# Expert gathers issued from rolled loops with a staged index, in place of 512 written-out gathers

## The chip, the cores and the metric

The kernel runs on one core of one Trainium2 chip. A core has five engines with instruction streams of their own: TensorE (PE in the rows), VectorE (DVE), ScalarE (ACT), GpSimd (POOL) and SyncE (SP). They share the on-chip memory SBUF and 16 DMA engines, and they order their work by semaphores. The metric is the device time of one launch in microseconds; the time quoted is the median of several executions. Lower is better.

## The reference, cut to what matters

Two transformer-like blocks run in a row over 256 tokens of width 2048, all in float32. The change touches one part of the first block, a mixture of 16384 tiny experts. Each token picks 128 of them (8 heads of 16), and each expert is one row of a table `u` and one row of a table `v`:

```
def peer(x, wq, subkeys, u_tab, v_tab):
    ...
    idx = jnp.take_along_axis(cand_i, pos, axis=-1)
    gate = jax.nn.softmax(top_s, axis=-1)
    ...
    def block(args):
        xt, it, gt = args
        ue = jnp.take(u_tab, it, axis=0)
        ve = jnp.take(v_tab, it, axis=0)
        act = jax.nn.gelu(jnp.einsum('td,ted->te', xt, ue).astype(f32), approximate=False)
        return jnp.einsum('te,ted->td', (gt * act).astype(ve.dtype), ve)
```

So 256 tokens times 128 experts times two tables are gathered, rows of 2048 floats (8 KB) each. The rest (an mLSTM and an S5 mixer before it, a second block with three attention kinds and a feed-forward layer behind it) is untouched.

## The kernel before, in words

**Tiling.** The 256 tokens are two tiles (`TT` = 2, index `t`) of 128 tokens, one token per SBUF partition. One gather brings, for one of the 128 choices `n`, the row that each of the 128 tokens wants: 128 rows of 8 KB, 1.0486 MB. It is an indirect DMA issued by GpSimd, whose index column is `idx[:, t, n:n+1]`. There are four passes `q` of 128 gathers: `q` = 0 (table u, tile 0), 1 (table v, tile 0), 2 (u, tile 1), 3 (v, tile 1).

**Buffers and order.** Gather `n` goes into row buffer `n % 8` of eight buffers (`GB` = 8, `rows_`), and bumps that buffer's semaphore `row_gathered`. VectorE takes the buffers in the same order. In a u pass (called dots below, `dots_of`, L1532) it multiplies the buffer by the tile's activations and sums, with one small copy of eight results (L1536) and a wait for it behind every eight. In a v pass (called sums, `sums_of`, L1546) it adds the buffer times a weight into the accumulator `res`, each step waiting for the step before. Both are hardware loops on VectorE, eight buffers a round. Behind each buffer VectorE bumps `rows_used` (`s_free`), and GpSimd may gather into that buffer again only then: gather `n` of pass `q` waits for `q * 128 + n + 1 - 8` of them.

**What stands between.** VectorE also works out which experts are wanted (routing). The first tile's routing is in four blocks of 32 choices, and dots alternate with routing steps; the second tile's routing lies between the dots and sums of the first. Early on, GpSimd's first eight gathers use only five buffers, because the others still hold scores (`first_gathers`). Meanwhile SyncE streams a weight matrix `w_ada` that TensorE multiplies (L439), and VectorE takes the result at one place between two rounds of dots (L1652).

**GpSimd's stream.** It is written out: 512 gathers behind each other, each with its wait (L1716, called from L1720 to L1747). GpSimd does nothing else in this phase. Before a block of gathers it waits for `experts_known` (`s_idx`).

The eight-row ring is set up by these lines:

```
rows_ = [place.take(D) for _ in range(GB)]
idx = place.take(TT, HK).bitcast(U32)
dots = small[:, 32:32 + GB]
s_row = [sem(f"row_gathered{i}") for i in range(GB)]
```

Of the kernel before, what the change touches and what calls it, by code (L numbers as in the profile page):

```python
# [11 lines left out]
U32 = mybir.dt.uint32  # L12
# [17 lines left out]
def build(nc, a, out):  # L30
# [19 lines left out]
    HK = PH * TOPK  # L50
# [19 lines left out]
    with ctx:  # L70
# [5 lines left out]
        def sem(name):  # L76

            phase_sems.append(nc.alloc_semaphore(name=name))
            return phase_sems[-1]
# [16 lines left out]
        def place_at(name, words, dt=F32, at=None):  # L96
            if at is None:
                at = taken_at[0]
                taken_at[0] += words
            assert at + words <= ARENA, (name, at + words - ARENA)  # L100
            return nc.alloc_sbuf_tensor_at(name, [P, words], dt, offset=base + 4 * at), at
# [16 lines left out]
        small, _ = place_at("small", 256)  # L118
# [185 lines left out]
        for s in SECTIONS:  # L304
            for n in range(s.n):
                g = len(reach)
# [157 lines left out]
        with nc.Block() as block:  # L464
            @block.gpsimd
            def _(g):
                n = [0]

                def then(ins):
                    ins.then_inc(s_const, 1)  # L470
                    n[0] += 1
                    g.wait_ge(s_const, n[0])
                g.memset(spread, 0.0).then_inc(s_sz, 1)
                g.memset(ident[:, :], 0.0)
                g.memset(ones[:, :], 1.0)
                g.memset(upto[:, :], 1.0)
                g.memset(maskG, 1.0)
                g.memset(maskB, 1.0)
                then(g.memset(causal[:, :], 0.0))
                g.affine_select(out=ident[:, :], in_=ident[:, :], compare_op=ALU.not_equal, fill=1.0, base=0,  # L480
                                pattern=[[-1, P]], channel_multiplier=1)
                g.affine_select(out=upto[:, :], in_=upto[:, :], compare_op=ALU.is_ge, fill=0.0, base=0,
                                pattern=[[1, P]], channel_multiplier=-1)
                g.affine_select(out=causal[:, :], in_=causal[:, :], compare_op=ALU.is_ge, fill=NEG, base=0,
                                pattern=[[-1, P]], channel_multiplier=1)
                then(g.affine_select(out=maskG, in_=maskG, compare_op=ALU.is_ge, fill=0.0, base=0,
                                     pattern=[[-HG, GP]], channel_multiplier=1))
                then(g.affine_select(out=maskG, in_=maskG, compare_op=ALU.is_ge, fill=0.0, base=HG - 1,
                                     pattern=[[HG, GP]], channel_multiplier=-1))
                for h in range(2):  # L490
                    m = maskB[h * PS:(h + 1) * PS]
                    then(g.affine_select(out=m, in_=m, compare_op=ALU.is_equal, fill=0.0, base=-h,
                                         pattern=[[-2, TC], [1, GP]], channel_multiplier=0))
# [580 lines left out]
        GB = 8  # L1074
        rows_ = [place.take(D) for _ in range(GB)]
# [3 lines left out]
        idx = place.take(TT, HK).bitcast(U32)  # L1079
# [2 lines left out]
        top = place.take(2 * PH, TOPK)  # L1082
        topi = place.take(2 * PH, TOPK)
        pos = place.take(2, HK)
        iota16 = small[:, 16:16 + TOPK]
        dots = small[:, 32:32 + GB]
        EARLY = 5
        QB = PH * 2 * HALF // NB
# [16 lines left out]
        HB = HK // GB  # L1105
# [43 lines left out]
        s_q, s_qT, s_qTc = sem("queries_taken"), sem("queries_transposed"), sem("queries_copied")  # L1149
        s_sc, s_scc, s_kept = sem("block_scores"), sem("block_scores_copied"), sem("early_scores_moved")  # L1150
        s_r, s_idx, s_e, s_g = sem("route_step"), sem("experts_known"), sem("gate_exponentials"), sem("activations")
        s_free = sem("rows_used")
        s_row = [sem(f"row_gathered{i}") for i in range(GB)]
        s_dv, s_gl = sem("dots_step"), sem("gelu_done")
        s_mtk, s_msum = sem("modulation_gathered"), sem("modulation_summed")
# [22 lines left out]
        with nc.Block() as block:  # L1178
# [529 lines left out]
            @block.gpsimd  # L1708
            def _(g):


                g.iota(iota16, pattern=[[1, TOPK]], base=0, channel_multiplier=0,
                       allow_small_or_imprecise_dtypes=True).then_inc(s_io, 1)

                def gather(t, table, n, dst):
                    g.indirect_dma_start(dst, None, a[table][0], bass.IndirectOffsetOnAxis(idx[:, t, n:n + 1], 0))\  # L1716
                     .then_inc(s_row[n % GB], 16)

                def first_gathers():

                    for n in range(2 * GB):
                        r = n % GB
                        if n < GB and r >= EARLY:
                            g.wait_ge(s_free, r - EARLY + 1)
                        if n >= GB and r < GB - EARLY:
                            g.wait_ge(s_free, EARLY + r + 1)
                        if n == GB + EARLY:
                            g.wait_ge(s_idx, 2)
                            g.wait_ge(s_sc, QB)
                            g.wait_ge(s_kept, 1)  # L1730
                        gather(0, "peer_u", n, rows_[r % EARLY if n < GB else r])

                def gathers(q, lo, hi):

                    for n in range(lo, hi):
                        g.wait_ge(s_free, q * HK + n + 1 - GB)
                        gather(q // 2, "peer_v" if q % 2 else "peer_u", n, rows_[n % GB])

                for b in range(QB):
                    g.wait_ge(s_idx, b + 1)  # L1740
                    if b == 0:
                        first_gathers()
                    gathers(0, max(2 * GB, HK // QB * b), HK // QB * (b + 1))
                for q in range(1, 2 * TT):
                    if q % 2 == 0:
                        g.wait_ge(s_idx, QB + 1)
                    gathers(q, 0, HK)  # L1747

            @block.scalar
            def _(act):  # L1750
# [443 lines left out]
        with nc.Block() as block:  # L2194
# [5 lines left out]
            def _(dve):  # L2200
# [9 lines left out]
                def copy_pair(m):  # L2210
                    dve.wait_ge(s_hT, m + 1)
                    for j in range(2):
                        _, _, dst, hh, gcol = heads[2 * m + j]
                        src = ps[m % 4][:, j * T:(j + 1) * T]
                        if gcol is None:
                            last = v.tensor_scalar(dst[:, hh, :], src, P ** -0.5 if dst is gqT else 1.0, None, ALU.mult)
                        else:
                            last = v.tensor_scalar(dst[:, hh, :], src, gains[:, gcol:gcol + 1], None, ALU.mult)
                    last.then_inc(s_hc[1], 1)
# [25 lines left out]
            @block.scalar  # L2245
            def _(act):
                def copy_pair(m):
                    act.wait_ge(s_hT, m + 1)
                    for j in range(2):
                        _, _, dst, hh, gcol = heads[2 * m + j]  # L2250
                        src = ps[m % 4][:, j * T:(j + 1) * T]
                        if gcol is None:
                            last = nc.scalar.mul(dst[:, hh, :], src, P ** -0.5 if dst is gqT else 1.0)
                        else:
                            last = nc.scalar.mul(dst[:, hh, :], src, gains[:, gcol:gcol + 1])
                    last.then_inc(s_hc[0], 1)

                gate_highs(act, 2)
                copy_pair(0)
                copy_pair(2)  # L2260
                gate_highs(act, 5)
                act.wait_ge(s_hs, hmarks["ss"])
                nc.scalar.activation(qk_ss, qk_ss, ACT.Sqrt).then_inc(s_hr, 1)
                for m in (4, 8, 12):
                    gate_highs(act, 7 + (m - 4) // 4)
                    copy_pair(m)
                    copy_pair(m + 2)
                gate_highs(act, 10)
# [945 lines left out]
```

## Time and profile before

| what | value |
|---|---|
| time, median of 3 executions | 3758.63 us (3755.48 to 3759.67) |
| the profiled execution | 3755.48 us, span 3753.5 us from first to last instruction |
| VectorE busy | 2548.7 us, 68% of the span |
| TensorE busy | 2302.4 us, 61% |
| GpSimd busy, as recorded | 1203.8 us, 32% |
| ScalarE busy | 805.9 us, 21% |
| software-generated DMA queue (the gathers) | 536.90 MB |
| hardware-generated DMA queue (weights and the rest) | 491.31 MB |

The gathers run from 637 us to 2048 us, and VectorE takes the last of them at about 2064 us. From there on TensorE's weight products lead. A row that names an engine, a line and an operation counts what is busy; "idle before" is how long the engine stood before such an instruction and what ended it. The record of a gather on GpSimd is rough: it can hold the time in which the gather, or the one behind it, waits for its semaphore, so the distance from one gather to the next says more than its length.

### The profile page before, as it was taken

The page shows a single profiled execution, that of the slowest core. Times are in us where ns is not written, and L with a number is a line of the kernel's source. Part 1 is how long each engine was busy: PE and PEld are TensorE (multiplying, and loading weights), DVE is VectorE, ACT ScalarE, POOL GpSimd, SP SyncE. Part 2 cuts the span into 40 slices and gives each one's busy share as a digit, 9 for nine tenths or more (in the row PEclk, how much of TensorE's full clock was granted, in tenths as well). Part 3 has the DMA queues.
Part 4 walks back from the last instruction along what each step waited for, and adds up shares of the span by engine and source line. Part 5 has one row for each costly group of instructions (what it writes and reads, how often), then busy time and mean ns, then how long its engine had stood idle before and what let it go on. Part 6 is the DMA issues. An engine that isn't in the chain of part 4 may idle for free. (4 is left out here: it accounts for less than half of the span.)

```text
span 3753.5 us, 27270 instructions
## 1 busy us (share of the span) xinstructions
PE 2302.4 (61%) x10328; PEld 1710.1 (46%) x10328; DVE 2548.7 (68%) x2400; ACT 805.9 (21%) x693; POOL 1203.8 (32%) x641
## 2 busy tenths in 40 slices
PE   7999899312000000000000899988899999999999
PEld 4444487100000000000000788876778878888887
DVE  3665547886999999999999444375856654444444
ACT  1001144000000000000000333244433433333333
POOL 1631000673768888788887000000000000000000
PEclk9999999655555555555555999899999999999999
DMA  6898465999989999999999455344465645555554
GB/s 197 287 347 309 162 221 194 383 414 407 374 356 394 422 420 407 422 422 422 422 422 395 147 195 195 123 141 129 130 210 190 247 157 190 188 188 188 200 195 161
DMA packets 332263, 1029.48 MB, mean 274 GB/s; under 512 B 35273, under 2 KB 35785, under 8 KB 264713
## 3 DMA queue, kind: packets, MB, share of 16 engines
q1 hardware_dynamic: 258440, 491.31, 38.7%
q0 software_dynamic: 73728, 536.90, 34.6%
q8 instruction: 61, 1.00, 0.1%
q14 instruction: 34, 0.27, 0.0%
HBM read 1021.28 MB, written 6.86 MB: 274 GB/s over the span
## 5 line engine op out<-in xcount | busy, mean ns | idle before, releaser
L383 DVE TENSOR_TENSOR slab_low<-ring,slab_high 128x2048 fp32r<-128x2048 f32 x240 | 550.1, 2292 | 675.1 <-ACT slab_high L376 674.9
L376 ACT CAST slab_high<-ring 128x2048 fp32r<-128x2048 f32 x304 | 580.1, 1909 | 1048.9 <-PE bank L362 799.3
L2103 PE MATMUL bank<-ident,nat 128*128 128x128 f32 x32 | 8.9, 433 | 1133.8 <-DVE nat L1591 1133.8
L1716 POOL DMA_INDIRECT pool<-in_peer_u,pool x256 | 518.6, 2026 | 511.4 <-DVE pool L1495 277.0
L1546 DVE SCALAR_TENSOR_TENSOR res<-pool,res 128x2048 f32<-128x2048 f32 x256 | 601.9, 2351 | 37.9 <-DVE pool L1552 0.6
L360 PE MATMUL bank<-slab_high,left_high 128*128 128x512 f32 x1568 | 615.6, 393 | 2.8 <-DVE slab_low L383 2.7
L362 PE MATMUL bank<-slab_high,left_low 128*128 128x512 f32 x1568 | 612.5, 391 | 0.0
L361 PE MATMUL bank<-slab_low,left_high 128*128 128x512 f32 x1568 | 612.4, 391 | 0.0
L1716 POOL DMA_INDIRECT pool<-in_peer_v,pool x256 | 556.3, 2173 | 101.0 <-issue 77.4
L1532 DVE CUSTOM_DVE_ANT_0 pool<-pool,nat 128x2048 f32<-128x2048 f32 x248 | 554.3, 2288 | 36.3 <-DMA pool<-in_peer_u,pool 27.0
L2103 PEld LDWEIGHTS bank<-ident,nat 128*128 128x128 f32 x32 | 5.7, 216 | 1137.5 <-DVE nat L1591 1137.5
L360 PEld LDWEIGHTS bank<-slab_high,left_high 128*128 128x128 f32 x1568 | 296.0, 189 | 65.2 <-issue 4.1
L362 PEld LDWEIGHTS bank<-slab_high,left_low 128*128 128x128 f32 x1568 | 295.8, 189 | 61.9
L361 PEld LDWEIGHTS bank<-slab_low,left_high 128*128 128x128 f32 x1568 | 296.1, 189 | 61.0
L439 PE MATMUL bank<-ring,pool 128*32 128x512 f32 x632 | 106.4, 782 | 229.1 <-DMA ring<-in_w_ada 225.0
L351 PE MATMUL bank<-ring,left_scratch 128*128 128x512 f32 x528 | 236.4, 603 | 5.2 <-PEq L705 4.1
L383 DVE TENSOR_TENSOR ring_low<-ring,slab_high 128x2048 fp32r<-128x2048 f32 x64 | 146.7, 2292 | 99.8 <-ACT slab_high L376 93.3
L2181 PE MATMUL bank<-slab_high,left_high 128*128 128x512 f32 x384 | 159.2, 415 | 39.5 <-DVE ring_low L383 25.6
L439 PEld LDWEIGHTS bank<-ring,pool 128*32 128x32 f32 x632 | 17.0, 122 | 311.0 <-DMA ring<-in_w_ada 275.3
L351 PEld LDWEIGHTS bank<-ring,left_scratch 128*128 128x128 f32 x528 | 99.9, 193 | 128.7 <-issue 128.3
L2182 PE MATMUL bank<-ring_low,left_high 128*128 128x512 f32 x384 | 155.6, 405 | 0.0
L2183 PE MATMUL bank<-slab_high,left_low 128*128 128x512 f32 x384 | 155.2, 404 | 0.0
(558 smaller groups left out, 2715.1 us busy)
## 6 DMA issues: line engine op xcount, KB each, us to landing
ring<-in_w_in SPq DMA_DIRECT2D x141, 1024.0 KB, 5.0
ring<-in_w_ffn_in SPq DMA_DIRECT2D x88, 1024.0 KB, 5.0
ring<-in_w_ada SPq DMA_DIRECT2D x79, 1024.0 KB, 9.8
ring<-in_w_ffn_out SPq DMA_DIRECT2D x44, 1024.0 KB, 5.0
ring<-in_w_out SPq DMA_DIRECT2D x32, 1024.0 KB, 5.1
pool<-in_w_ada SPq DMA_DIRECT2D x17, 1024.0 KB, 8.7
ring<-in_peer_wq SPq DMA_DIRECT2D x16, 1024.0 KB, 5.1
ring<-in_w_br_gla SPq DMA_DIRECT2D x8, 1024.0 KB, 5.1
```

The costliest lines, as they stand in the source:

```text
L351: last = nc.tensor.matmul(o, raw_left[:, k0 + k, t * P:(t + 1) * P], slot(g)[:, k, :], start=start and k == 0, stop=stop and k == KS - 1)
L360: nc.tensor.matmul(o, lh, high[:, part, k, :], start=first, stop=False)
L361: nc.tensor.matmul(o, lh, low[:, part, k, :], start=False, stop=False)
L362: last = nc.tensor.matmul(o, ll, high[:, part, k, :], start=False, stop=final)
L376: nc.scalar.copy(high[:, n % PARTS], ring[:, g % SLOTS]).then_inc(high_done, 1)
L383: eng.tensor_tensor(dst, ring[:, g % SLOTS], high[:, n % PARTS].bitcast(F32), ALU.subtract)\
L1532: v.tensor_tensor_reduce(out=rows_[r], in0=rows_[r], in1=nat[:, t, :], scale=1.0, scalar=0.0, op0=ALU.mult, op1=ALU.add, accum_out=dots[:, ...
L1546: v.scalar_tensor_tensor(res[:, t, :], rows_[r], actv[:, t, bass.ds(i * GB + r, 1)], res[:, t, :], ALU.mult, ALU.add).then_inc(s_free, 1)
L1716: g.indirect_dma_start(dst, None, a[table][0], bass.IndirectOffsetOnAxis(idx[:, t, n:n + 1], 0))\
L2181: nc.tensor.matmul(o, lh, hi, start=first, stop=False)
L2182: nc.tensor.matmul(o, lh, ring_low[:, g % SLOTS, k, :], start=False, stop=False)
L2183: return nc.tensor.matmul(o, ll, hi, start=False, stop=final)
```

## The change

GpSimd's part alone is edited. Each gather no longer reads its index from the big index array. Instead eight index columns at a time (a half) are first copied by GpSimd into one of two small stages of eight columns in the tile `small`; GpSimd waits for that copy, and the eight gathers read their index columns from the stage. With an index that always lies at a fixed place, the gathers of a pass become a hardware loop over pairs of halves (16 gathers a turn), in place of being written out. Each gather gets an increment of a new semaphore `gathers_let_go` ahead of it, that nobody waits for; the wait for a free row sits on this increment. The number of gathers, their order, their buffers and the rows that each must wait for stay as they are.

```
@@ -1082,6 +1082,7 @@
         pos = place.take(2, HK)
+        stage = small[:, 0:2 * GB].bitcast(U32)
         iota16 = small[:, 16:16 + TOPK]
@@ -1149,7 +1150,7 @@
-        s_free = sem("rows_used")
+        s_stage, s_free, s_turn = sem("indices_staged"), sem("rows_used"), sem("gathers_let_go")
@@ -1712,39 +1713,54 @@
-                def gather(t, table, n, dst):
-                    g.indirect_dma_start(dst, None, a[table][0], bass.IndirectOffsetOnAxis(idx[:, t, n:n + 1], 0))\
-                     .then_inc(s_row[n % GB], 16)
-
-                def first_gathers():
-
-                    for n in range(2 * GB):
-                        r = n % GB
-                        if n < GB and r >= EARLY:
-                            g.wait_ge(s_free, r - EARLY + 1)
-                        if n >= GB and r < GB - EARLY:
-                            g.wait_ge(s_free, EARLY + r + 1)
-                        if n == GB + EARLY:
-                            g.wait_ge(s_idx, 2)
-                            g.wait_ge(s_sc, QB)
-                            g.wait_ge(s_kept, 1)
-                        gather(0, "peer_u", n, rows_[r % EARLY if n < GB else r])
-
-                def gathers(q, lo, hi):
-
-                    for n in range(lo, hi):
-                        g.wait_ge(s_free, q * HK + n + 1 - GB)
-                        gather(q // 2, "peer_v" if q % 2 else "peer_u", n, rows_[n % GB])
-
+                def gather(src, r, dst, st):
+                    g.sem_inc(s_turn, 1)
+                    g.indirect_dma_start(dst, None, src, bass.IndirectOffsetOnAxis(st[:, r:r + 1], 0))\
+                     .then_inc(s_row[r], 16)
+
+                def first_halves():
+
+                    for p in range(2):
+                        st = stage[:, p * GB:(p + 1) * GB]
+                        g.tensor_copy(st, idx[:, 0, p * GB:(p + 1) * GB]).then_inc(s_stage, 1)
+                        g.wait_ge(s_stage, p + 1)
+                        for r in range(GB):
+                            ...
+                            gather(a["peer_u"][0], r, rows_[r % EARLY if p == 0 else r], st)
+
+                def half(q, i, p):
+                    t = q // 2
+                    src = (a["peer_v"] if q % 2 else a["peer_u"])[0]
+                    st = stage[:, p * GB:(p + 1) * GB]
+                    g.tensor_copy(st, idx[:, t, bass.ds(i * (2 * GB) + p * GB, GB)]).then_inc(s_stage, 1)
+                    for r in range(GB):
+                        if r == 0:
+                            g.wait_ge(s_stage, i * 2 + (q * HB + p + 1))
+                        g.wait_ge(s_free, i * (2 * GB) + (q * HK + p * GB + r + 1 - GB))
+                        gather(src, r, rows_[r], st)
+
+                def halves(q, lo, hi):
+                    with g.Fori(lo, hi) as i:
+                        half(q, i, 0)
+                        half(q, i, 1)
+
+                per = HB // 2 // QB
                 for b in range(QB):
                     g.wait_ge(s_idx, b + 1)
                     if b == 0:
-                        first_gathers()
-                    gathers(0, max(2 * GB, HK // QB * b), HK // QB * (b + 1))
+                        first_halves()
+                    halves(0, max(1, per * b), per * b + per)
                 for q in range(1, 2 * TT):
                     if q % 2 == 0:
                         g.wait_ge(s_idx, QB + 1)
-                    gathers(q, 0, HK)
+                    halves(q, 0, HB // 2)
```

Before, GpSimd's queue at the end of the first tile's dots and in the sums behind them held gathers alone. `rows_used` is the wait for a free row buffer, `experts_known` the wait for the routing.

```order
L1716 DMA pool<-in_peer_u,pool 128x2048 [waits rows_used] x31
L1716 DMA pool<-in_peer_v,pool 128x2048 [waits rows_used] x128
L1716 DMA pool<-in_peer_u,pool 128x2048 [waits rows_used,experts_known]
L1716 DMA pool<-in_peer_u,pool 128x2048 [waits rows_used] x127
L1716 DMA pool<-in_peer_v,pool 128x2048 [waits rows_used] x128
```

After the change one turn of such a loop holds this, on the same engine; shown are the loop's head and the seam between its two halves. The tile `pool` is now only the source of the copy and the target of the rows; the index comes from `small`.

```order
L1742 COPY small<-pool 128x8
L1745 ISA
L1746 REGISTER_ALU [waits indices_staged]
L1718 DMA pool<-in_peer_u,small 128x2048 [waits rows_used]
L1746 REGISTER_ALU
L1718 DMA pool<-in_peer_u,small 128x2048 [waits rows_used]
...
L1742 ISA
L1742 COPY small<-pool 128x8
L1745 REGISTER_ALU
L1746 REGISTER_ALU [waits indices_staged]
L1718 DMA pool<-in_peer_u,small 128x2048 [waits rows_used]
```

A copy now stands behind each eighth gather, and the gather behind it cannot be let go before the copy is done. ISA and REGISTER_ALU rows are register arithmetic for the loop's wait values.

At the start of the phase the written-out beginning was this before:

```order
L1716 DMA pool<-in_peer_u,pool 128x2048 [waits experts_known]
L1716 DMA pool<-in_peer_u,pool 128x2048 x4
L1716 DMA pool<-in_peer_u,pool 128x2048 [waits rows_used] x6
L1716 DMA pool<-in_peer_u,pool 128x2048 x2
L1716 DMA pool<-in_peer_u,pool 128x2048 [waits early_scores_moved,qkv_taken,experts_known]
```

and is this now, with the two copies of the first sixteen indices:

```order
L1725 COPY small<-pool 128x8 [waits experts_known]
L1718 DMA pool<-in_peer_u,small 128x2048 [waits indices_staged]
L1718 DMA pool<-in_peer_u,small 128x2048 x4
L1718 DMA pool<-in_peer_u,small 128x2048 [waits rows_used] x3
L1725 COPY small<-pool 128x8
L1718 DMA pool<-in_peer_u,small 128x2048 [waits indices_staged,rows_used]
L1718 DMA pool<-in_peer_u,small 128x2048 [waits rows_used] x2
```

The very first gather, which waited for the routing alone, now stands behind a copy; the ninth stands behind a copy and its free row. On the other four engines nothing moved.

## Rows read from the trace of the kernel before

**Rows 1.** The page's costliest groups, gathered rows and VectorE's use of them.

```profile
L1546 DVE SCALAR_TENSOR_TENSOR res<-pool,res 128x2048 f32<-128x2048 f32 x256 | 601.9, 2351 | 37.9 <-DVE pool L1552 0.6
L1716 POOL DMA_INDIRECT pool<-in_peer_v,pool x256 | 556.3, 2173 | 101.0 <-issue 77.4
L1532 DVE CUSTOM_DVE_ANT_0 pool<-pool,nat 128x2048 f32<-128x2048 f32 x248 | 554.3, 2288 | 36.3 <-DMA pool<-in_peer_u,pool 27.0
```

**Rows 2.** Windows: engine busy and count, clock, DMA share, GB/s; tile 1.

```profile
1451.00:1742.00 291.00, 4.46 (x16) 2.86 (x16) 280.01 (x274) 6.90 (x12) 238.57 (x119) 0.50 1.01 417
1742.00:2065.00 323.00, 0.00 (x0) 0.00 (x0) 303.97 (x131) 5.97 (x6) 265.07 (x122) 0.50 0.99 413
```

**Rows 3.** Timeline in the second sums: start, length, instruction, idle before.

```profile
1797.95 32.30 DVE L1546 SCALAR_TENSOR_TENSOR res<-pool,res 128x2048 f32<-128x2048 f32 x13
1798.92 2.19 POOL L1716 DMA_INDIRECT pool<-in_peer_v,pool  x1 [0.30 <-issue]
```

**Rows 4.** Timeline in the second dots, one round of eight.

```profile
1608.29 0.17 DVE L1536 COPY pool<-small 128x8 f32 x1
1608.93 2.29 DVE L1532 CUSTOM_DVE_ANT_0 pool<-pool,nat 128x2048 f32<-128x2048 f32 x1 [0.47 <-DVE pool L1536]
1609.26 2.78 POOL L1716 DMA_INDIRECT pool<-in_peer_u,pool  x1 [0.30 <-issue]
...
1612.34 1.91 POOL L1716 DMA_INDIRECT pool<-in_peer_u,pool  x1 [0.30 <-issue]
...
1627.49 2.29 DVE L1532 CUSTOM_DVE_ANT_0 pool<-pool,nat 128x2048 f32<-128x2048 f32 x1 [0.46 <-DVE pool L1536]
```

**Rows 5.** Timeline of GpSimd at the first gathers, which wait for nothing.

```profile
643.21 0.93 POOL L1716 DMA_INDIRECT pool<-in_peer_u,pool  x1 [0.31 <-issue]
```

**Rows 6.** Line 1716, and the DMA issues of 1742 to 2065 us.

```profile
DMA to landing us min/median/max: 6.9/11.5/23.4
...
pool<-in_peer_v,pool POOLq DMA_INDIRECT x122, 14.9
```

**Rows 7.** Timeline and one window around VectorE's wait for the ada product.

```profile
915.88 1.94 PE L439 MATMUL bank<-ring,pool 128*32 128x512 f32 x8 [9.80 <-DMA ring<-in_w_ada]
...
930.08 0.69 DVE L1652 TENSOR_TENSOR pool<-pool,bank 128x512 f32<-128x512 f32 x1 [32.33 <-PE bank L439]
...
900.00:905.00 5.00, 0.86 (x6) 0.20 (x8) 0.00 (x0) 0.00 (x0) 0.00 (x0) 0.50 1.03 416
```

**Rows 8.** Waits by engine and line, 1076 to 2065 us, VectorE.

```profile
DVE pool L1532 <- DMA pool<-in_peer_u,pool: 2.3, 13, 0.2
```

**Rows 9.** Timeline where GpSimd and VectorE use SBUF together, large operations.

```profile
147.07 1.89 DVE L1007 TENSOR_TENSOR pool<-pool,res 128x1024 f32<-128x1024 f32 x1
...
147.84 2.90 POOL L699 TENSOR_TENSOR parts_scratch<-parts_scratch 128x1024 f32<-128x1024 f32 x1
...
148.88 2.94 DVE L1008 TENSOR_TENSOR pool<-pool,res 128x1024 f32<-128x1024 f32 x1
```

**Rows 10.** The two lines' own answers: least, median and longest.

```profile
L1008 DVE TENSOR_TENSOR pool<-pool,res x8: 1210/1215/2946, 131.3 to 323.8; 128x1024 f32<-128x1024 f32 x8
...
L699 POOL TENSOR_TENSOR parts_scratch<-parts_scratch x8: 1922/1928/2908, 106.4 to 287.8; 128x1024 f32<-128x1024 f32 x8
```

**Rows 11.** Timeline and line 890, small GpSimd operations beside VectorE.

```profile
78.95 1.03 POOL L797 TENSOR_TENSOR parts_scratch<-parts_scratch,res 128x32 f32<-128x32 f32 x1
79.94 1.24 POOL L798 TENSOR_TENSOR parts_scratch<-parts_scratch,res 128x32 f32<-128x32 f32 x1
81.14 0.27 POOL L799 TENSOR_TENSOR parts_scratch<-parts_scratch,res 128x32 f32<-128x32 f32 x1
...
L890 DVE TENSOR_TENSOR res<-res,small x2: 1225/1255/1285, 78.6 to 79.8; 128x1024 f32<-128x1024 f32 x2
```

**Rows 12.** Lines 488, 705 and 1546: a small GpSimd operation, sequencer work.

```profile
L488 POOL TENSOR_SCALAR_AFFINE_SELECT small<-small x1: 192/192/192, 3.7 to 3.7; 128x8 f32<-128x8 f32 x1
...
L705 POOLq COMPARE_BRANCH  x1: 33/33/33, 113.1 to 113.1; - x1
...
L705 POOLq EVENT_SEMAPHORE  x2: 17/17/17, 113.3 to 113.4; - x2
...
L1546 DVEq FUSED_REGOPS  x248: 57/57/57, 1119.7 to 2061.9; - x124
```

**Rows 13.** The page's DMA queue of instructions.

```profile
q14 instruction: 34, 0.27, 0.0%
```

More of the change, by code:

```diff
@@ L1733, in gathers @@
-                def gathers(q, lo, hi):
-                    for n in range(lo, hi):
-                        g.wait_ge(s_free, q * HK + n + 1 - GB)
-                        gather(q // 2, "peer_v" if q % 2 else "peer_u", n, rows_[n % GB])
+                def gather(src, r, dst, st):
[8 more added lines that the diff above has]
+                        for r in range(GB):
+                            if p == 0 and r >= EARLY:
+                                g.wait_ge(s_free, r - EARLY + 1)
+                            if p == 1 and r < GB - EARLY:
+                                g.wait_ge(s_free, EARLY + r + 1)
+                            if p == 1 and r == EARLY:
+                                g.wait_ge(s_idx, 2)
+                                g.wait_ge(s_sc, QB)
+                                g.wait_ge(s_kept, 1)
+                            gather(a["peer_u"][0], r, rows_[r % EARLY if p == 0 else r], st)
```

## The prediction, made before the changed kernel was run

> **What bounds the kernel now.** I read the page's costliest groups first, then windows over the phase of the gathers, then timelines of single rounds, and last the places where GpSimd and VectorE meet. In the groups [rows 1] VectorE spends 601.9 us on 256 sums of 2351 ns and 554.3 us on 248 dots of 2288 ns. GpSimd's gathers look as busy (2173 ns each), but that number misleads. The first gathers, which wait for nothing, take 0.93 us and stand 0.31 us apart [rows 5], so GpSimd can issue one per 1.24 us. In a run of sums one step of VectorE is (32.30 - 2.35) / 12 = 2.50 us, and GpSimd's record is 2.19 + 0.30 = 2.49 us: it moves in VectorE's step, waiting inside its record [rows 3]. A round of eight dots is 1627.49 - 1608.93 = 18.56 us, 2.32 us a gather [rows 4].
>
> The DMA engines are the second limit, and a near one. In the second tile they are busy 0.99 to 1.01 of the time and move 413 to 417 GB/s [rows 2]. A gather of 1.0486 MB takes 2.52 us at 416 GB/s [rows 7], or a little less at the best stretches. So VectorE's sums (2.50 us) and the DMA are even, dots (2.32 us) ask for more than the DMA gives, and the ring of eight buffers carries the difference. That it does is shown by the waits: in the whole stretch from 1076 us on VectorE waits for gathered rows 13 times, 2.3 us in total [rows 8]. VectorE leads, with the DMA right behind, and GpSimd has about half of each step free.
>
> **The slack of a gather.** In the sums VectorE's step that began at 1797.95 ends at 1800.30; the gather record in which that wait lies ends at 1798.92 + 2.19 = 1801.11, 0.81 us later [rows 3]. The data lands 14.9 us after issue in this stretch, but 6.9 us where no backlog stands in the queue [rows 6]. So some 8.0 us of the landing is time in the queue: a gather issued up to 8 us late finds the DMA still busy with earlier ones and lands when it would have landed. Lateness below that costs nothing by itself.
>
> **The change part by part.**
>
> *The loop's own work on GpSimd*: one increment per gather (17 ns), register arithmetic (57 ns on VectorE, the nearest row), one branch per 16 gathers (33 ns) [rows 12]. That makes 0.08 us a gather, to 1.32 us, against a step of 2.32 us or more. It is hidden by GpSimd's free half. Its cost on the path is 0; without that cover it would be 512 x 0.08 = 41 us. The wait now sits on an increment ahead of the gather, so the gather may be prepared only after the wait: at worst the end comes 1.24 us after the row is free in place of 0.81. That 0.4 us is far below 8 us: 0.
>
> *The copy, as lateness.* It stands behind each eighth gather and ahead of the next. GpSimd operations of 128x8 take 0.19 us [rows 12]. The copy may have to wait for a VectorE operation to end, up to 2.35 us; the next gather's row comes free at the end of just that operation, so the gather is late by the copy and its own preparation, 0.19 + 0.4 + 0.1 = 0.7 us, and the second gather behind it (a step later, needing 1.32 us) is on time again. 0.7 us against 8 us: 0. Queued behind the copy are only gathers; who waits for those is VectorE, one ring later.
>
> *The copy, as a load on VectorE.* This is the term that I charge. Where both engines read SBUF, they take turns. VectorE's L1008 takes 1.21 us alone and took 2.94 us at 148.88, and GpSimd's L699 takes 1.93 us alone and 2.90 us beside it [rows 9, 10]. L699 began at 147.84, and 150.74 - 1.93 = 148.81 is when it can have started to work, as L1007 drew to its end. Turns are also taken between two VectorE operations that stand back to back, so a copy is served at the next boundary. For small ones: two additions of 128x32 on GpSimd took 1.03 and 1.24 us beside VectorE's L890, where 0.27 us is the length alone; the two L890 took 1.225 and 1.285 us [rows 11]. GpSimd waited about 0.8 us for VectorE, VectorE 0.06 us for GpSimd. I take 0.06 us per copy. The bounds: 0, if the copy slips into the gap between two sums (2.50 - 2.35 = 0.15 us) or the 0.64 us from the small copy to the next dot [rows 4]; and the whole 0.19 us of a 128x8 operation.
>
> The Trainium skill, "SBUF — State Buffer", section "Who interferes with whom", says that a VectorE instruction with two SBUF inputs and a GpSimd instruction that reads SBUF hold the shared read interface exclusively, each for its whole instruction. By that rule the charge is the upper bound, 0.19 us; the large operations agree with it [rows 9, 10], the small ones show a third of it [rows 11].
>
> *How many count.* There are 64 copies. The first ten serve choices 0 to 79 of the first dots. At 930.08 VectorE has waited 32.33 us for TensorE, which waits for `w_ada`, while the DMA is at 1.03 [rows 7]; the bytes to be moved before that point do not change, so what VectorE loses earlier comes out of that wait. That leaves 6 + 16 + 16 + 16 = 54 copies. 54 x 0.06 = 3.2 us; bounds 0 and 54 x 0.19 = 10.3 us. In the late second dots VectorE waits for data anyway [rows 8] and could swallow up to 2.3 us; I leave that in the margin.
>
> *What goes away.* The written-out stream must be fetched: this queue moved 0.27 MB over the whole kernel [rows 13], 0.65 us of DMA at 416 GB/s. Nothing in GpSimd's rows waits for it. Gain at most 0.6 us; I take 0.
>
> *The start.* The first gather comes up to a copy and a VectorE operation later. It is issued at 637, five gathers are out by 645, and the first dot is at 666; hidden.
>
> **Sum.** 3755.48 + 3.2 = 3758.7 us for the profiled execution. That one was the fastest of three; it stands 3.15 us below the median, 3758.63. Against the median the sum is 3761.8 us, 0.08% slower, which a measurement of this kernel can't tell from no change: 0.2% is 7.5 us.
>
> **The rivals.**
>
> *A, the copy holds VectorE while it waits for its own engine (slower).* The copy stands right behind a gather whose descriptors take 0.93 us. If part of GpSimd starts the copy and holds the read side while the rest is still at descriptors, VectorE's next operation waits until both are done. Price: in sums 0.93 - 0.15 = 0.78 us x 32, in dots 0.93 - 0.64 = 0.29 us x 22, so 25 + 6.4 = 31 us: 3790. It decides as soon as the hold is longer than the gap. For it: the copy comes just when VectorE's gap begins. Against: in rows 11 two small operations in a row cost VectorE 0.06 us, though no row has one behind a gather. The same sentence of "SBUF — State Buffer" would allow this, since it says that the pair is held for the full instruction.
>
> *B, the copy starves (much slower).* If VectorE's dots never let GpSimd in between, a copy that misses the gap waits for the round's end, and eight gathers start together. A round is then 6.9 + 7 x 2.5 + 2.3 + 0.85 = 27.6 us in place of 18.56, for 22 rounds: 199 us, 3960. Rows 9 speak against it, since L699 got in between L1007 and L1008.
>
> *C, the whole-instruction charge plus loop effects (slower, small).* 54 x 0.19 = 10.3 us and a microsecond or two where the ring is empty: 3770. For it: the page's rule. Against: rows 11.
>
> *D, a gain.* The shorter stream would have to free something that VectorE or the DMA waits for. I find only the 0.6 us of fetching. A result below 3751 would need a cause that is not in these rows. That the change does not do what it says I hold for out of the question in the order of instructions: the same 512 gathers with the same waits are there.
>
> **How the numbers follow.** My forecast (0 to 6 us slower) has 0.70. C has 0.14, A and milder forms of it 0.08, B 0.02, D and other gains 0.06. The bound of 0.2% lies at 3751.1 and 3766.1. Faster: most of D, 0.05. Slower: A, B and two thirds of C, 0.20. Within 0.2%: the rest, 0.75. The range runs from 3753 (a gain of noise size) to 3782 (the milder half of A).
>
> **What would show it.** Right: 64 copies on GpSimd, most recorded at 1 to 2.5 us (waiting for VectorE), dots and sums with the same median (2288 and 2351 ns) and at most 64 of them longer by 0.1 us; median landing time in the sums near 14.9 us or a little less; the 32 us wait at L1652 changed by the copies' few tenths only; the last sum ends 2 to 5 us later than now. Wrong: VectorE rows of 2.9 us and more behind each eighth gather (A), VectorE waiting for gathered rows in each round (B), or GpSimd gathers more than 2.3 us apart when rows are free, which would mean that the loop's work is larger than 0.08 us.

## The result and the profile after

The changed kernel took 3823.43 us (median of 4 runs, 3817.75 to 3833.57; three further ones lie between 3822.23 and 3826.17), the kernel before 3757.12 us (4 runs, 3755.48 to 3759.67). The ratio is 1.0179, with a 95% interval of 1.0164 to 1.0195: 66 us slower. The prediction said 3761.8 us with a range that ended at 3782, so it was wrong by far. The profiled execution after has a span of 3821.6 us, 68.1 us more than before.

The page's groups after, which answer to [rows 1] (busy us, mean ns of one, idle time before it and what ended it):

```profile
L1547 DVE SCALAR_TENSOR_TENSOR res<-pool,res 128x2048 f32<-128x2048 f32 x256 | 603.2, 2356 | 84.2 <-DMA pool<-in_peer_v,small 54.6
...
L1533 DVE CUSTOM_DVE_ANT_0 pool<-pool,nat 128x2048 f32<-128x2048 f32 x248 | 557.6, 2291 | 53.6 <-DMA pool<-in_peer_u,small 44.1
...
L1718 POOL DMA_INDIRECT pool<-in_peer_v,small x256 | 551.9, 2156 | 104.8 <-issue 68.3
```

These rows close the account. VectorE's idle time before the sums went from 37.9 to 84.2 us (+46.3), before the dots from 36.3 to 53.6 us (+17.3), and the busy time of the two rows grew by 1.3 + 3.3 = 4.6 us. Together that is 68.2 us against 68.1 us of span. Not all of the 4.6 us is slower work. Two dots that follow each other without a wait overlap in the records (a step of 2.21 us, a length of 2.29 us), and a dot that has to wait no longer overlaps, which raises the busy time by itself. Added up one by one, all 512 records together grew by 2.1 us (my count). That is all that the forecast's charge can be held against; the other 66 us are waits, most of them for gathered rows.

Where it happens is seen from the ends of the four passes (a pass is 128 choices, dots or sums of one tile; I took the ends from VectorE's timeline):

| kernel | end of first dots | first sums | second dots | second sums |
|---|---|---|---|---|
| before | at 1090.5 | 337.2 us | 313.9 us | 322.7 us |
| after | at 1092.4 | 352.7 us | 333.7 us | 355.0 us |

The loss grows from pass to pass: 1.9, 15.5, 19.8 and 32.3 us. (The 1.9 us is hardly more than the spread: in the kernel before and the runs below in which GpSimd makes no copies in this stretch, the first dots end between 1090.4 and 1092.0.) The DMA engines are not what got slower: they had less to move. The windows of [rows 2] read after:

```profile
1451.00:1742.00 291.00, 4.46 (x16) 2.86 (x16) 268.74 (x260) 9.68 (x13) 248.92 (x126) 0.50 0.99 403
1742.00:2065.00 323.00, 0.00 (x0) 0.00 (x0) 274.90 (x134) 5.38 (x5) 278.88 (x131) 0.50 0.96 378
```

In the second window the DMA moved 378 GB/s in place of 413, VectorE was busy 274.90 us in place of 303.97, and GpSimd 278.88 us in place of 265.07. TensorE's granted clock is the same 0.50 of full speed, which is 1.2 GHz. The new limit is on GpSimd's side. The waits and the gathers' landing over the second sums (1779 to 2134 us; least, median and longest):

```profile
DVE res L1547 <- DMA pool<-in_peer_v,small: 37.1, 41, 3.0
POOL pool L1718 <- POOL small L1742: 13.3, 15, 0.9
```

```profile
L1718 POOL DMA_INDIRECT pool<-in_peer_v,small x126: 934/2192/3067, 1777.5 to 2122.4; - x126
...
DMA to landing us min/median/max: 6.7/8.8/13.8
```

The landing fell from 14.9 us [rows 6] to 8.8 us. The backlog in the queue, which was to cover a late gather, was used up, and VectorE waits 41 times. Gathers that come 0.7 us late now and then can't do that; they must have come later and later. I worked it out from the trace: the start of the n-th gather's record less the end of VectorE's use n - 8, which frees its buffer. I call this the gather's lateness. Before, its median is 1.11 to 1.12 us in every pass. After, it is 3.15 us in choices 88 to 127 of the first dots, then 6.1, 8.4 and 11.2 us in the next three passes. VectorE reaches a buffer again 7 uses after it was freed, 7 x 2.50 = 17.5 us; 11.2 us of lateness and the 6.7 us of the quickest landing are 17.9 us. There the ring is empty. The growth comes in steps: in the first sums after, four halves in a row (choices 56 to 87) have a lateness of 3.6, 6.1, 8.6 and 11.2 us, 2.5 us more behind each copy. Up to 8.6 us VectorE still waits for no row of them; at 11.2 us it does.

Why the lateness isn't made good is seen in one round of the second sums after (start, length, instruction, idle before in brackets):

```profile
1808.26 9.89 DVE L1547 SCALAR_TENSOR_TENSOR res<-pool,res 128x2048 f32<-128x2048 f32 x4 [1.02 <-DMA pool<-in_peer_v,small]
1808.36 3.07 POOL L1718 DMA_INDIRECT pool<-in_peer_v,small  x1 [0.30 <-issue]
1811.73 2.19 POOL L1718 DMA_INDIRECT pool<-in_peer_v,small  x1 [0.30 <-issue]
1813.92 1.79 POOL L1742 COPY small<-pool 128x8 uint32 x1
1816.59 2.40 POOL L1718 DMA_INDIRECT pool<-in_peer_v,small  x1 [0.89 <-POOL small L1742]
...
1846.43 0.94 POOL L1718 DMA_INDIRECT pool<-in_peer_v,small  x1 [0.30 <-issue]
1847.67 0.94 POOL L1718 DMA_INDIRECT pool<-in_peer_v,small  x1 [0.30 <-issue]
1848.02 2.35 DVE L1547 SCALAR_TENSOR_TENSOR res<-pool,res 128x2048 f32<-128x2048 f32 x1 [2.71 <-DMA pool<-in_peer_v,small]
```

Taken one by one, the four sums end at 1810.61, 1813.11, 1815.66 and 1818.16. GpSimd's records end at 1811.43, 1813.92, 1815.71 and 1818.99: a gather 0.8 us behind the end of a sum, the copy 0.05 us behind one. Each has the end of one sum to itself, the copy too. These rows were free long before, so it isn't the free row that they wait for. Where VectorE stands idle (1845.31 to 1848.02) gathers take 0.94 us and follow each other at 1.24 us. I call the end of a VectorE operation at which GpSimd is served a **turn**. Eight gathers need eight turns for eight sums, and there are just eight. The copy makes nine.

### The profile page after: what moved, and what is told of

Same layout as the page of the kernel before. It is cut to its first block and busy times, and to the rows that moved or that the text cites. A ratio compares the mean times of both kernels' runs of the same rounds, so it can differ in the third digit from the quotient of the medians.

```text
span 3821.6 us, 28505 instructions
## 1 busy us (share of the span) xinstructions
PE 2299.6 (60%) x10328; PEld 1707.5 (45%) x10328; DVE 2554.1 (67%) x2400; ACT 806.0 (21%) x693; POOL 1285.7 (34%) x705
## 5 line engine op out<-in xcount | busy, mean ns | idle before, releaser
L1547 DVE SCALAR_TENSOR_TENSOR res<-pool,res 128x2048 f32<-128x2048 f32 x256 | 603.2, 2356 | 84.2 <-DMA pool<-in_peer_v,small 54.6
L1533 DVE CUSTOM_DVE_ANT_0 pool<-pool,nat 128x2048 f32<-128x2048 f32 x248 | 557.6, 2291 | 53.6 <-DMA pool<-in_peer_u,small 44.1
L1718 POOL DMA_INDIRECT pool<-in_peer_u,small x256 | 516.6, 2018 | 225.7 <-DVE small L1533 113.5
L1718 POOL DMA_INDIRECT pool<-in_peer_v,small x256 | 551.9, 2156 | 104.8 <-issue 68.3
```

The source lines that it names most:

```text
L1533: v.tensor_tensor_reduce(out=rows_[r], in0=rows_[r], in1=nat[:, t, :], scale=1.0, scalar=0.0, op0=ALU.mult, op1=ALU.add, accum_out=dots[:, ...
L1547: v.scalar_tensor_tensor(res[:, t, :], rows_[r], actv[:, t, bass.ds(i * GB + r, 1)], res[:, t, :], ALU.mult, ALU.add).then_inc(s_free, 1)
L1718: g.indirect_dma_start(dst, None, src, bass.IndirectOffsetOnAxis(st[:, r:r + 1], 0))\
```

## The experiments

Theories: *turns* (above); *loop* (the written-out stream or the loop's increments and waits cost it); *latency* (the wait for the copy's end delays the gather, whatever the copy reads). All times are against runs of the kernel before on the same chip.

**The copies alone, without the loop.** The stream stays written out, with 64 copies:

```
+ def stage_indices(t, n):
+     if n % GB == 0:
+         g.tensor_copy(stage[:, n % (2*GB):n % (2*GB) + GB],
+                       idx[:, t, n:n + GB]).then_inc(s_stage, 1)
+         staged[0] += 1
+         g.wait_ge(s_stage, staged[0])
- ... IndirectOffsetOnAxis(idx[:, t, n:n + 1], 0)
+ ... IndirectOffsetOnAxis(stage[:, n % (2*GB):n % (2*GB) + 1], 0)
```

> The kernel before, its 512 gathers still written out, with one thing of the change: ahead of each eighth gather GpSimd copies eight index columns to a stage, waits for the copy, and the eight gathers read the stage. No loop, no extra increment. Theory (turns): a gather on GpSimd is served once per VectorE operation with two SBUF inputs, and a copy needs a turn of its own, so eight gathers and a copy need nine turns where VectorE's round has eight; the gathers fall behind until VectorE must wait. Then this alone costs what the whole change cost: 50 to 75 us more than before, of which 28 to 36 us in the last sums. Rival (loop): the hardware loop, its register work and the wait on the increment make GpSimd late; then this kernel is within 8 us of before.

Measured: 3817.98 us, ratio 1.0164 (1.0147 to 1.0181). Nearly the whole loss is there without a loop. It isn't told apart from the changed kernel's 1.0179. One forecast of *turns* missed here: the second sums are 20.6 us longer, not 28 to 36; the second dots are 25.2 us longer and the first sums 13.3.

```profile
1852.38 17.38 DVE L1547 SCALAR_TENSOR_TENSOR res<-pool,res 128x2048 f32<-128x2048 f32 x7 [1.74 <-DMA pool<-in_peer_v,small]
...
1858.05 1.78 POOL L1720 COPY small<-pool 128x8 uint32<-128x8 uint32 x1
1860.10 3.01 POOL L1725 DMA_INDIRECT pool<-in_peer_v,small  x1 [0.27 <-POOL small L1720]
```

The third of the seven sums in this row ends at 1859.78; the copy ends 0.05 us later. The gather begins 0.27 us after that, takes 3.01 us and ends at 1863.11, 0.83 us behind the fourth sum (1862.28). Two turns again.

**The loop without GpSimd's copies.** Loops, increments and the stage as in the change, but from the third half on ScalarE does the copies:

```
- g.tensor_copy(st, idx[...]).then_inc(s_stage, 1)
+ ...
+ act.wait_ge(s_free, max((h - 1) * GB, GB + 1))
+ nc.scalar.copy(stage[:, h % 2 * GB:(h % 2 + 1) * GB],
+                idx[:, q // 2, m * GB:(m + 1) * GB]).then_inc(s_stage, 1)
```

> The changed kernel with its loops, increments and stages, but the copies of all halves from the third on are made by ScalarE, which is nearly idle here; GpSimd copies only the first two. Theory (turns): GpSimd has eight operations per round of eight again; within 6 us of before, and a gather starts about 1.1 us after its row is free throughout. Rival (loop): the loop is all there, so it is still 50 us or more slower than before. Rival (stage): if reading the index from the stage tile, or waiting for the stage, is what costs, it is slower by tens of us too.

Measured: 3758.72 us, ratio 1.0005 (0.9996 to 1.0015). *Loop* is out. A start of about 1.1 us behind the free row throughout had been expected, and that did not hold: in the second sums the median lateness is 3.35 us (my count), while VectorE's idle time stays as before (18.7 us in that pass). The run with the increments alone, below, shows the same slip. Once a turn is lost in these sums it isn't won back until VectorE pauses, and a lateness that doesn't grow costs nothing.

**VectorE's sums with one SBUF input**, in the kernel before and in the changed one:

```
- v.scalar_tensor_tensor(res[:, t, :], rows_[r], actv[...], res[:, t, :],
-                        ALU.mult, ALU.add).then_inc(s_free, 1)
+ v.tensor_reduce(dots[:, r:r + 1], rows_[r], AX, ALU.add).then_inc(s_free, 1)
```

> The kernel before, with VectorE's weighted addition in the sums (two SBUF inputs) replaced by a row reduction of the gathered rows (one SBUF input), so the expert sums are left out. Theory (turns): with one input VectorE does not hold GpSimd up, so in the sums a gather whose row is free is recorded at about 0.93 us and not at 2.19. The sums then run at the pace of the DMA or of the reduction, whichever is slower: 2.3 to 2.5 us a row, so 0 to 25 us less than before in each. Rival: the 2.19 us of a gather is a wait for the DMA's descriptor ring or for its row; then the records stay near the pace of the rows.

> The changed kernel with the same replacement: one SBUF input for VectorE in the sums, the expert sums left out. Theory (turns): copies are recorded at about 0.2 us in the sums, the gathers catch up there, and both sums passes take within 3 us of the time they take with the same replacement in the kernel before; the dots passes, untouched, still cost about 20 us more, so the whole is 15 to 28 us above that kernel. Rival (the copy's own latency of 0.2 us and 0.9 us behind it, or the loop): the sums stay slower by 15 and 32 us as in the changed kernel, and the whole by 60 us or more.

Measured: 3744.22 and 3754.77 us, one run each. The first with the loads as before, then the changed one:

```profile
1849.67 2.29 DVE L1546 TENSOR_REDUCE small<-pool 128x1 f32<-128x2048 f32 x1 [0.20 <-DMA pool<-in_peer_v,pool]
1849.75 0.94 POOL L1715 DMA_INDIRECT pool<-in_peer_v,pool  x1 [1.56 <-DVE small L1546]
```

```profile
1862.85 0.19 POOL L1741 COPY small<-pool 128x8 uint32 x1
1863.78 2.29 DVE L1547 TENSOR_REDUCE small<-pool 128x1 f32<-128x2048 f32 x1 [0.19 <-DMA pool<-in_peer_v,small]
1864.40 0.96 POOL L1717 DMA_INDIRECT pool<-in_peer_v,small  x1 [1.36 <-DVE small L1547]
```

Beside an operation of about the same length (2.29 us) a gather takes 0.94 us and a copy 0.19 us, and both sums passes are as long with the copies as without (324.5 against 323.3 us, 320.9 against 320.9). In the second sums after, the median lateness is 0.81 us in place of 11.2. So what holds GpSimd is the two-input operation, and without it the copy is free. (The two operations also differ in what they write, 2048 columns against one, and no run separates that from the second input; but a memset that only writes SBUF isn't held by the two-input sums, as shown below.) The Trainium skill, "SBUF — State Buffer", section "Who interferes with whom", says that a VectorE instruction with two SBUF inputs contends with a GpSimd instruction that reads SBUF and that `tensor_reduce` never does; the trace agrees, with 2.19 and 0.94 us. The difference of 10.5 us between the two kernels was expected at 15 to 28 us: a miss in size, as far as single runs tell (runs of one kernel lie up to 9 us apart). The dots, which have two inputs in both, cost 5.2 us more in the second pass.

**The copy twice**, each with its wait:

```
+ for k in range(2):
+     g.tensor_copy(...).then_inc(s_stage, 1); staged[0] += 1
+     g.wait_ge(s_stage, staged[0])
```

> The written-out kernel with the copy of each half made twice, one behind the other with a wait between (128 copies). Theory (turns): a round of eight gathers needs ten turns, so the loss more than doubles, since the pauses of the routing that swallowed part of the first 64 copies are used up: 130 to 200 us slower than before, 60 to 75 us of it in the last sums. Rival (a fixed price per staged half, by the first wait or by reading the stage tile): the second copy adds little, 60 to 80 us in all.

Measured: 3837.40 us, ratio 1.0215 (1.0195 to 1.0236), 81 us slower. That is a miss for *turns* as I had put it, one turn for every read.

```profile
1848.66 12.39 DVE L1547 SCALAR_TENSOR_TENSOR res<-pool,res 128x2048 f32<-128x2048 f32 x5 [0.45 <-DMA pool<-in_peer_v,small]
...
1851.83 2.03 POOL L1721 COPY small<-pool 128x8 uint32<-128x8 uint32 x2
1854.39 2.50 POOL L1727 DMA_INDIRECT pool<-in_peer_v,small  x1 [0.53 <-POOL small L1721]
```

Both copies together take 2.03 us, where one takes 1.78. The second one, though it waits for the first, begins 0.06 us behind it and slips into its turn. In the second sums the loss is 31 us, where 60 to 75 were expected.

**Half as many copies**, of 16 indices each:

```
- if n % GB == 0:
+ if n % (2 * GB) == 0:
-     ... idx[:, t, n:n + GB]
+     ... idx[:, t, n:n + 2 * GB]
```

> The written-out kernel with one copy of 16 index columns ahead of each sixteenth gather (32 copies, the same number of columns). Theory (turns): 17 turns per 16 gathers; the pauses swallow a larger part than of 64 copies, so 15 to 30 us slower than before. Rival (the columns copied are the cost): as much as with 64 copies of eight, 61 us.

Measured: 3783.57 us, ratio 1.0072 (1.0052 to 1.0092), 27 us slower, so 0.85 us a copy (0.6 to 1.1 by the interval) against 61.4 / 64 = 0.96 us in the written-out kernel. The loss goes with the number of copies, not with the number of columns.

**A memset in the copy's place**, with the same wait; the gathers take their indices from `idx` as in the kernel before:

```
- g.tensor_copy(stage[...], idx[:, t, n:n + GB]).then_inc(s_stage, 1)
+ g.memset(stage[...], 0).then_inc(s_stage, 1)
```

> The written-out kernel with a memset of 128x8 (GpSimd writes SBUF and reads nothing) in the place of each copy, with the same wait; the gathers read their index from the big array as before. Theory (turns, read side): only GpSimd operations that read SBUF wait for VectorE's two-input operations, so the memset takes about 0.1 us and the time is within 8 us of before. Rival (turns for every GpSimd operation, or the wait itself): 50 to 70 us slower like the copy.

Measured: 3758.00 us, ratio 1.0004 (0.9995 to 1.0014).

```profile
1866.27 0.12 POOL L1720 MEMSET small<- 128x8 uint32 x1
1866.66 2.11 POOL L1725 DMA_INDIRECT pool<-in_peer_v,pool  x1 [0.27 <-POOL small L1720]
```

An operation that writes SBUF and reads none takes 0.12 us beside the same sums, and the gather behind its wait (0.27 us, as behind the copy) is served on time. *Latency* by itself is out; the read matters.

**One increment ahead of every gather**, nothing else:

```
+ g.sem_inc(s_turn, 1)
  g.indirect_dma_start(...)
```

> The kernel before with the increment ahead of each of the 512 gathers, the wait for the row on it, and nothing else. Both theories: within 6 us of before; the start of a gather behind its free row moves by less than 0.5 us.

Measured: 3758.20 us, ratio 1.0005 (0.9995 to 1.0015). The wait that moved to an increment costs no time. But the start of a gather moved by more than the 0.5 us that was expected at most. At four places, 106 gathers apart, a gather in the kernel before starts 1.75 us behind its free row in place of 1.12, and loses nothing (my count). With the increment ahead the same four lose a turn, with no copy anywhere, and in the sums the lateness then stays at 3.61 us until a pause of VectorE. So the increment does make a few gathers late, and the ring covers it.

**The copy early.** 64 copies, each put ahead of the fifth gather of the half before, so that no gather waits for a fresh copy; four stages in place of two:

```
+ if n % GB == 4 and h + 1 < 2 * TT * HB:
+     ...
+     copy_half(h + 1)
+ if n % GB == 0:
+     g.wait_ge(s_stage, h + 1)
```

> The written-out kernel with 64 copies as in e1, but each copy stands in the middle of the half before (ahead of its fifth gather), in one of four stages, so that no gather waits for a copy just made: the wait for it comes four gathers later. Theory (turns): it is not the wait that costs but the turn that the copy takes from a gather; 45 to 65 us slower than before. Rival (latency behind the copy: the gather is late because it waits for the copy's completion): most of the loss goes, within 15 us of before. Between the two lies the case that a gather queued right behind the copy is served in the same turn, as the second copy was in e5: 15 to 40 us.

Measured: 3764.19 us, ratio 1.0022 (1.0012 to 1.0031), 8 us slower. The same 64 reads cost 8 us and not 61: against *turns* as written, and what *latency* had said.

```profile
1862.77 1.78 POOL L1720 COPY small<-pool 128x8 uint32<-128x8 uint32 x1
1864.71 0.96 POOL L1736 DMA_INDIRECT pool<-in_peer_v,small  x1 [0.16 <-DVE res L1547]
1865.97 1.87 POOL L1736 DMA_INDIRECT pool<-in_peer_v,small  x1 [0.30 <-issue]
```

The copy ends at 1864.55. The gather, which has nothing to wait for, begins 0.16 us later and takes 0.96 us: it is served in the copy's turn. The next gather is in step again, and no turn is lost. So it goes in 29 of the 30 such gathers of the two sums passes. In the dots it often does not:

```profile
1505.93 1.45 POOL L1720 COPY small<-pool 128x8 uint32<-128x8 uint32 x1
...
1507.25 2.29 DVE L1533 CUSTOM_DVE_ANT_0 pool<-pool,nat 128x2048 f32<-128x2048 f32 x1
1507.54 2.84 POOL L1736 DMA_INDIRECT pool<-in_peer_u,small  x1 [0.16 <-DVE small L1533]
```

The next dot has begun at 1507.25, before the copy ends at 1507.38, and the gather is held until that dot is done. This happens in 10 of the 16 rounds of the second dots. The lateness there rises to 7.7 us and the pass is 2.4 us longer; VectorE's pauses between rounds give most of it back. In the passes the median lateness stays at 1.1 to 3.7 us, and VectorE's idle time in the second sums is 18.7 us, as before. What is left of the 8 us is in part VectorE's own durations, 604.3 us of sums against 601.9.

Together: the memset has the wait without the read, and costs nothing; the early copy has the read without the wait, and costs 8 us; both together cost 61 us. **The cause is the pair: a copy that reads SBUF, and a wait for its end in front of the next gather. The copy is served at the end of a VectorE operation, the wait keeps the gather back until VectorE's next operation has begun, and the gather gets only the turn behind that one.** None of these kernels is faster than the one before.

That VectorE's next start decides, and not the delay as such, is seen in the run with the copies alone. There the gather always begins 0.27 us behind the copy in the sums passes (29 gathers; two more come late for another reason). Mostly VectorE's next sum begins 0.12 us or less after the copy's end, and the gather takes 3.0 us: 22 times. But where VectorE has to wait for a row, its next sum begins later, and then the same gather is served at once: 7 times, each with at least 0.24 us from the copy's end to the sum.

```profile
1900.89 2.40 DVE L1547 SCALAR_TENSOR_TENSOR res<-pool,res 128x2048 f32<-128x2048 f32 x1
1901.56 1.78 POOL L1720 COPY small<-pool 128x8 uint32<-128x8 uint32 x1
1903.61 0.96 POOL L1725 DMA_INDIRECT pool<-in_peer_v,small  x1 [0.27 <-POOL small L1720]
1903.88 2.35 DVE L1547 SCALAR_TENSOR_TENSOR res<-pool,res 128x2048 f32<-128x2048 f32 x1 [0.58 <-DMA pool<-in_peer_v,small]
```

Over the sums passes of the changed kernel and of the four runs with two-input sums and copies on GpSimd, I counted the 107 gathers that begin within 1 us of a copy. The 38 whose record begins before VectorE's next sum, or at most 0.07 us behind its start, take 0.96 us; the 69 that begin 0.10 us or more behind it are held until it ends. There is no exception. That is also one reason why the loss isn't a full turn a copy: a gather that finds VectorE waiting for a row is served at once.

Open is the same bound in the dots, where two copies and a gather were held that began only 0.01 to 0.06 us behind the start of a dot. Nor was a gather tried in a loop that takes its index from a fixed place, without any copy on any engine.

## Why the prediction was wrong

*The slack of a gather* is half right. A lateness below about 8 us costs nothing, as the run with ScalarE's copies shows at 3.35 us and the first sums after at 8.6 us, and the landing fell from 14.9 to 8.8 us. But it was right for one gather only, and no term of the sum asked what the next 64 would do.

*The copy, as lateness* is the step that failed. It took GpSimd as able to issue one gather per 1.24 us, from the first gathers [rows 5], where VectorE ran nothing but short routing operations (0.07 to 0.29 us each), and so let "the second gather behind it" be on time again. Beside two-input operations the pace is one per VectorE operation, 2.50 us in the sums, however late the gather is. Nothing is made good except where VectorE idles. The copy with its wait loses a turn, 16 times a pass: 16 x 2.50 = 40 us in the second sums at the most, of which 32.3 us came out as time. "GpSimd has about half of each step free" was true for time, as the memset shows, and untrue for reads of SBUF.

The trace in hand could have told it. In [rows 3] the gather's record ends 0.81 us behind a sum, and I read that as the wait for the buffer freed by that sum. It was not: the lateness of 1.12 us in the kernel before says that the record began 1.12 us after its row was free. The other reading was in the rows too: [rows 5] show 0.93 us, and a wait of 1.26 us *inside* a record, in place of ahead of it, is unlike a wait for a free buffer. Beside one-input sums that same wait stands ahead of the record: 1.56 us in the brackets, and 0.94 us of record. And [rows 9], [rows 11] had shown GpSimd held by VectorE, which I used for VectorE's loss of 0.06 us and not for GpSimd's of a whole turn.

*The copy, as a load on VectorE*, the one term charged, was right in size where it applies: in the changed kernel a sum at whose end a copy is served takes 2.40 us in place of 2.35, so 0.05 us a copy against the 0.06 charged. The median dot with a copy at its end takes 2.29 us, no more than before. In total it is 2.1 us against 3.2. The copies themselves look as foretold:

```profile
L1742 POOL COPY small<-pool x62: 196/1766/2093, 693.7 to 2102.1; 128x8 uint32 x60, 128x8 uint32<-128x8 uint32 x2
```

*The loop's own work* and the wait on the increment were right at 0 us of time, shown by the increment alone and by the loop with ScalarE's copies; that it leaves every gather on time was not. *What goes away* was right: the instruction queue of [rows 13] moved 0.27 MB after as before.

```profile
q14 instruction: 33, 0.27, 0.0%
```

*The wait for the ada product* of [rows 7] did not take up what was lost ahead of it, as the prediction had it. VectorE reached the wait 1.3 us later and it then lasted 0.6 us longer, since the product came 1.9 us later; the first dots end later by the same 1.9 us. Why the product was late was not looked into, and it is within the spread named above:

```profile
DVE pool L1653 <- PE bank L439: 33.0, 1, 33.0
```

Of the rivals, A asked for VectorE to be held by the copy for 0.78 us at a time; its dots and sums grew by 3 and 5 ns in the mean, so no. C's 10 us is not reached by that load either. D did not come. B came nearest in kind, GpSimd kept out by VectorE. But it saw the copy wait for a round's end, with all eight gathers behind it at once, and priced that at 199 us. What happened is milder and adds up: one turn each, taken from the ring's reserve until that is gone. The sign that the prediction had named, gathers more than 2.3 us apart where rows are free, stands in the trace, for a cause I had not given it.

## What to carry over

When an engine seems to have half its time free beside a busy one, ask what it has free: time, or turns at what both use; compare the length of its record while the other is idle with that while it works. Before an SBUF read is put on GpSimd beside two-input VectorE work in steady step, count GpSimd's reads against VectorE's operations, and if one must be added, put it where nothing waits for it at once, or where VectorE pauses. A delay is harmless only if the engine can catch up: check the pace that it has under load, not the one it has alone.

## What the runs showed of the hardware

- A gather whose indices lie in SBUF takes 0.94 us on GpSimd beside an idle VectorE or a one-input reduction of 2.29 us, and 2.19 us (one per 2.50 us) beside a two-input operation of 2.35 us.
- A 128x8 copy on GpSimd takes 0.19 us in the first case and 1.77 us (median) in the second, ending 0.04 to 0.05 us behind a VectorE operation in the sums; a memset of the same size takes 0.12 us beside the same operation.
- A second read close behind the first shares its turn if it begins before VectorE's next two-input operation or, in the sums, at most 0.07 us behind its start: a copy behind a copy (2.03 us for both), and 38 gathers behind a copy (0.96 us). From 0.10 us on it is held for that whole operation (69 gathers, 2.4 to 3.1 us).
- VectorE's side of it: a sum of 2.35 us takes 2.40 us when a copy is served at its end.
